# Two transformer blocks on one core: weight pieces issued as the ones before them land, and modulation rows and scan results placed in later levels of the token steps

## The reference

```python
mod = jax.nn.silu(c) @ ada_w[l] + ada_b[l]
sh1, sc1, g1, sh2, sc2, g2 = [m[:, None, :] for m in jnp.split(mod, 6, axis=-1)]
hx = modulate(rms_norm(x, norm1_g[l]), sh1, sc1)

def step(S, inp):
    r_t, w_t, kk_t, b_t, v_t, k_t = inp
    sa = jnp.einsum("bhvk,bhk->bhv", S, kk_t)
    S = (S * w_t[:, :, None, :] - sa[..., None] * b_t[:, :, None, :]
         + v_t[..., None] * k_t[:, :, None, :])
    return S, jnp.einsum("bhvk,bhk->bhv", S, r_t)

for d in range(N_DIR):
    state, y = wkv_scan(init[d], rh, to_heads(decay), kk, kk * to_heads(a), vh, to_heads(k_d),
                        reverse=(d == 1))
    y_sum = y if y_sum is None else y_sum + y
```

## Time and profile before

| | us |
|---|---|
| median of 3 runs | 1566.41 (1563.55 to 1569.16) |
| the profiled execution, its own time | 1571.56 |
| its span, first to last instruction | 1570.0 |
| PE busy | 1489.1 |
| DVE busy | 920.6 |
| ACT busy | 597.5 |
| POOL busy | 272.7 |
| mean granted TensorE clock, share of full speed | 0.962 |

### The profile page before, as it was taken

The page is one execution under the profiler, slowest core; times in us unless marked ns, Lnnn a source line. Parts: engine busy times, 40 slices in busy tenths (PEclk is TensorE's granted clock), DMA queues, the critical chain, the costliest instruction groups (busy, mean ns, idle before and its releaser), DMA issues.

```text
span 1570.0 us, 35522 instructions
## 1 busy us (share of the span) xinstructions
PE 1489.1 (95%) x14858; PEld 1227.3 (78%) x14858; DVE 920.6 (59%) x1499; ACT 597.5 (38%) x1037; POOL 272.7 (17%) x290
## 2 busy tenths in 40 slices
PE   5999988999999989999999998998989999999997
PEld 3788865788899777887777887877878888888885
DVE  4424245588667748888886224767565655555222
ACT  4422344435342534444443223546664222322221
POOL 0000023565352010111111121000021111111110
PEclk9999997789879999999999999999999999999999
DMA  9232201233220222232223222221112232232221
GB/s 372 96 109 81 81 0 50 63 95 103 81 64 4 83 81 81 81 107 82 105 87 104 92 92 81 98 72 55 59 50 87 102 107 91 96 107 92 93 92 72
DMA packets 38987, 139.15 MB, mean 89 GB/s; under 512 B 3152, under 2 KB 3664, under 8 KB 38480
## 3 DMA queue, kind: packets, MB, share of 16 engines
q1 hardware_dynamic: 38720, 135.24, 25.4%
q10 hardware_dynamic: 144, 2.10, 0.3%
HBM read 135.22 MB, written 2.10 MB: 87 GB/s over the span
## 4 chain that ended last, share of the span: by engine, by line
PE 79%; DVE 13%; ACT 3%; issue 3%; DMA 1%; ACTq 0%; DVEq 0%; SPq 0%
PE bank L722 56%; PE bank L904 9%; DVE ffn_sb L3159 5%; PE bank L731 2%; PE bank L668 2%; PE bank L998 1%; DVE w_up L2587 1%; PE bank L1070 1%; PE bank L1010 1%; DMA arena<-w 1%; PE bank L935 1%; PE bank L661 1%; ACT w_up L1681 1%; ACT arena L2177 1%; DVE w_in L2587 1%
## 5 line engine op out<-in xcount | busy, mean ns | idle before, releaser
L722 PE MATMUL bank<-hf_hi,w_up 128*128 128x512 f32 x1376 | 424.0, 389 | 0.0
L722 PEld LDWEIGHTS bank<-hf_hi,w_up 128*128 128x128 f32 x1376 | 258.3, 188 | 53.2
L722 PE MATMUL bank<-hf_lo,w_up 128*128 128x512 f32 x688 | 269.1, 391 | 4.6 <-DVE w_up L2587 4.6
L722 PE MATMUL bank<-act_hi,w_down 128*128 128x512 f32 x704 | 216.7, 389 | 0.0
L904 PEld LDWEIGHTS bank<-arena 64*64 64x64 f32 x4224 | 161.1, 154 | 31.6 <-issue 19.3
L904 PE MATMUL bank<-arena 64*64 64x32 f32 (+1 forms) x4224 | 172.4, 237 | 7.8 <-DVE arena L2814 2.5
L1681 ACT ACTIVATE w_up<-ring 128x1024 fp32r<-128x1024 f32 x87 | 91.9, 1058 | 215.7 <-PE bank L722 215.7
L2587 DVE TENSOR_TENSOR w_up<-ring,w_up 128x1024 fp32r<-128x1024 f32 x87 | 106.8, 1229 | 97.0 <-ACT w_up L1681 97.0
L722 PEld LDWEIGHTS bank<-hf_lo,w_up 128*128 128x128 f32 x688 | 129.1, 188 | 36.1 <-DVE w_up L2587 8.8
L3159 DVE SCALAR_TENSOR_TENSOR ffn_sb<-ffn_sb 128x512 f32<-128x512 f32 x176 | 151.5, 861 | 5.4
L722 PEld LDWEIGHTS bank<-act_hi,w_down 128*128 128x128 f32 x704 | 132.1, 188 | 27.3
(11 more groups left out here) (350 smaller groups left out, 2388.8 us busy)
## 6 DMA issues: line engine op xcount, KB each, us to landing
ring<-w SPq DMA_DIRECT2D x76, 1024.0 KB, 4.8
ring<-w SPq DMA_DIRECT2D x32, 704.0 KB, 4.0
ring<-w SPq DMA_DIRECT2D x64, 256.0 KB, 3.0
arena<-w SPq DMA_DIRECT2D x8, 1024.0 KB, 18.2
x<-xT SPq DMA_DIRECT2D x1, 2048.0 KB, 10.2
x<-xT ACTq DMA_DIRECT2D x1, 2048.0 KB, 8.4
outT<-x SPq DMA_DIRECT2D x4, 512.0 KB, 2.7
arena<-ctxT SPq DMA_DIRECT2D x1, 1024.0 KB, 18.4
```

The lines of the kernel that those rows point to most:

```text
L722: ins = mm(out, w[:, a, k, :], of_block(b, k0 + k), start=first and k == 0 and m == 0, stop=last and k == n - 1 and m == 2)
```

## The change

Three things are changed.

1. `load_paced` no longer goes by the levels of the scan. The 8 pieces of a step go round by round: the first piece of either slot waits until PE has used the slot, and every further piece waits until the piece before it in its own slot has landed. The two slots take turns, so at most two pieces are under way. `pace` is gone.
2. The PE loop over n = 2 to 10 is split in two. For n = 2 to 6 the rows move back: `ada_part(n, 0)` behind `nx(m, 0, 5)`, `ada_part(n, 1)` behind `dx(m, 0, 5)`, `ada_select(n)` behind `dx(m, 0, 6)`. For n = 7 to 10, which have no rows, the results move back: `results(n, 0)` behind `dx(m, 0, 4)`, `results(n, 1)` behind `dx(m, 0, 5)`.
3. ACT's `first_result(n, 1)` moves ahead of `ada_row_out(n)` and `state_padded(m, 1)`.

```diff
-            def load_paced(g, at, m, u):
-
-                sp.wait_ge(s["product"], DONE[g - 2])
-                to = ring[:, g % 2, :].rearrange("p (c n) -> p c n", c=2)
+            def load_paced(m):
+
                 for e in range(PARTS):
-                    step, l = pace(m, u, e)
-                    sp.wait_ge(s[("nx_mm0", "dx_mm0")[l % 2]], 5 * step + l // 2 - 1)
                     c, half = e // 2, slice(KB * P // 2 * (e % 2), KB * P // 2 * (e % 2 + 1))
-                    sp.dma_start(to[:, c, half], w8[2 * at + c][:, half]).then_inc(s[f"slot_in{g % 2}"], 16)
+                    for u in range(2):
+                        g = PACED[2 * m + u]
+                        at = 21 + g - SLOT["ADA2"]
+                        to = ring[:, g % 2, :].rearrange("p (c n) -> p c n", c=2)
+                        if e == 0:
+                            sp.wait_ge(s["product"], DONE[g - 2])
+                        else:
+                            sp.wait_ge(s[f"slot_in{g % 2}"], 16 * (LANDED[g] - PARTS + e))
+                        sp.dma_start(to[:, c, half], w8[2 * at + c][:, half]).then_inc(s[f"slot_in{g % 2}"], 16)
...
-            for n in range(NCC - 2, NC - 1):
+            for n in range(NCC - 2, 7):
                 m, q = n + 1, n + 2
...
                 results(n, 1)
-                ada_part(n, 0)
                 dx(m, 1, 4)
                 nx(m, 0, 5)
-                ada_part(n, 1)
+                ada_part(n, 0)
                 nx(m, 1, 5)
                 dx(m, 0, 5)
+                ada_part(n, 1)
                 dx(m, 1, 5)
                 nx(m, 0, 6)
+                nx(m, 1, 6)
+                dx(m, 0, 6)
                 ada_select(n)
+                dx(m, 1, 6)
+            for n in range(7, NC - 1):
...
+                nx(m, 0, 4)
+                turned(m, 1)
+                nx(m, 1, 4)
+                dx(m, 0, 4)
+                results(n, 0)
+                dx(m, 1, 4)
+                nx(m, 0, 5)
+                nx(m, 1, 5)
+                dx(m, 0, 5)
+                results(n, 1)
+                dx(m, 1, 5)
+                nx(m, 0, 6)
                 nx(m, 1, 6)
                 dx(m, 0, 6)
                 dx(m, 1, 6)
...
                 tok_out(m, 0)
+                first_result(n, 1)
                 ada_row_out(n)
                 state_padded(m, 1)
-                first_result(n, 1)
                 state_padded(m, 0)
```

More of the change, by code:

```diff
@@ L630, in _ @@
             for m in range(8):
-                for u in range(2):
-                    g = PACED[2 * m + u]
-                    load_paced(g, 21 + g - SLOT["ADA2"], m, u)
+                load_paced(m)
             sp.wait_ge(s["bh0"], 2 * NCC)
@@ L1271, in _ @@
                 results(n, 1)
-                ada_part(n, 0)
                 dx(m, 1, 4)
                 nx(m, 0, 5)
-                ada_part(n, 1)
+                ada_part(n, 0)
                 nx(m, 1, 5)
                 dx(m, 0, 5)
+                ada_part(n, 1)
                 dx(m, 1, 5)
                 nx(m, 0, 6)
+                nx(m, 1, 6)
+                dx(m, 0, 6)
                 ada_select(n)
+                dx(m, 1, 6)
+            for n in range(7, NC - 1):
+                m, q = n + 1, n + 2
+                nx(m, 0, 2)
+                updates(n, 0)
+                nx(m, 1, 2)
+                scores(q, 0)
+                dx(m, 0, 2)
+                dx(m, 1, 2)
+                state_terms(n, 0)
+                if n == NC - 2:
+                    gate_products(0, 1)
+                updates(n, 1)
+                nx(m, 1, 3)
+                nx(m, 0, 3)
+                scores(q, 1)
+                dx(m, 1, 3)
+                turned(m, 0)
+                dx(m, 0, 3)
+                state_terms(n, 1)
+                if n == NC - 2:
+                    gate_products(1, 2)
+                nx(m, 0, 4)
[10 more added lines that the diff above has]
+                nx(m, 0, 6)
                 nx(m, 1, 6)
```

## The result

The changed kernel takes 1570.33 us, the median of 20 runs (1563.94 to 1574.71), against 1563.74 us for the kernel before (20 runs, 1556.07 to 1569.68). The ratio is 1.0038, with a 95% interval of 1.0023 to 1.0053: 0.4% slower, where 1555 and faster was forecast. The profiled execution took 1572.13 us, of which 1570.4 are the span; before, these were 1571.56 and 1570.0. Its mean granted clock is 0.966, and it was 0.962.

A forecast was written before the change was run, and what follows sets the result against it. PE, busy 1489.1 of 1570.0 us, was taken as the bound. 1571.6 - 19.2 (clock) + 2.0 + 3.2 (order) = 1557.6; for the median run 1557.6 or 1552.4, middle 1555 (chance 0.75), range 1548 to 1565.

The forecast's parts named there:

- the order: Moved PE groups in steps 2 to 10: +2.0 us in steps 2 and 3, 0 in 4 to 6, +3.2 in 7 to 10.
- the clock term: Wide products late in scan steps keep PE's clock from falling to half: -19.2 us, bounds 0 and -19.2.
- one long fall: Profiled execution lies 5.2 us above the median run, about one long clock fall; if so, the median had fewer to lose.
- no stretch of 13.6 us at 0.50 between 340 and 520: Sign in the changed profile that the forecast is right: no such long half-clock stretch of PE there.
- Order, steps 7 to 10: Second moved result group adds 1.1 us, level 5 gains 0.3: +0.8 a step, 3.2 in four; bounds -0.3 and 2.2 a step.
- PE's idle time ahead of `nx(m, 1, 5)`: Sign in the changed profile: PE idle some 0.5 us there in steps 7 to 10.
- the results lose their cover: Rival: DVE ends level 4, so moved results are exposed on PE in full; 1577 if the clock gains nothing; chance 0.04.
- Order, steps 2 and 3: Second row product comes where nobody waits and adds 1.0 us a step, +2.0 in all; bounds 0 and 1.0 a step.
- About 1.2 us: Sign in the changed profile: PE idle this long before `dx(m, 1, 4)` of steps 2 and 3.
- Order, steps 4 to 6: Rows change places with groups PE has to do in any case, no new wait: 0.
- Pieces: Steady pair of weight loads, no row product waits: 0, between -0.8 and +0.8 us a step, 4 us either way.
- The rival of the pieces that hold up PE's instructions: Two pieces always under way cost 0.8 us more in each of five steps, 1559; chance 0.04.

The follow-up runs named there:

- r_pieces: Kernel before with only the change's new issue of the weight pieces, PE's order as before: 1565.5 us, ratio 1.0025.
- r_old_pieces: The change with weight pieces issued as before and POOL writing direction 1's decayed result rows behind the keys: 1557.2 us, ratio to before 0.9954.
- r_pool: The change with POOL's decayed result rows of direction 1 moved behind the keys: 1560.4 us, ratio to before 0.9983.
- r_back1: Kernel before with results of steps 7 to 10 moved, but `results(n, 1)` right behind `results(n, 0)`, POOL's order as before: 1562.3 us, ratio 1.0005.
- r_results_pool: Kernel before with the results of steps 7 to 10 moved and POOL's direction 1 result rows behind the keys: 1559.8 us, ratio 1.0004.
- r_best: Kernel before with rows of steps 4 to 6 and results of steps 7 to 10 moved, POOL's direction 1 result rows behind the keys: 1561.1 us, ratio 0.9979.
- r_results: Kernel before with only the results of steps 7 to 10 moved, and ACT's order there as in the change: 1567.7 us, ratio 1.0032.
- r_rows: Kernel before with only the rows of steps 2 to 6 moved: 1561.8 us, ratio 1.0000.
- r_rows4: Kernel before with only the rows of steps 4 to 6 moved: 1559.9 us, ratio 0.9982.
- r_late1: Against r_results, `results(n, 1)` three groups later still in steps 7 to 10: 1581.6 us, ratio to before 1.0115, 6 runs.

## Why the prediction was wrong

The terms of the sum came to -19.2 for the clock and +5.2 for the order, -14.0; the medians moved by +6.6. Of these 20.6 us the clock term holds 16.1 and the rest 4.6. Two steps failed, the clock's size and the order in steps 7 to 10, and they don't weigh the same. With the clock term at its measured -3.1, the forecast order alone gives +2.1: the oversized clock term is enough to turn the sign. With only the order as measured, the sum would still be -9.4.

**Clock, -19.2 us: the direction was right, the size was not.** The time at half clock (twice 1 minus the mean clock, times the span) is 102.8 us on average over before's 99 runs, and 94.1 in the change's 20. At 0.36 us each that gives back 3.1 us. Two things went wrong here. I took the falls of one execution as fixed to their places, but r_pieces has the same order of products and none of the three long falls. The profiled execution, at 0.962, was below before's mean of 0.9671. The prediction saw that it might be "one long fall" off and still took off two of three. And it did not see that the change would bring new falls. Its sign of being right, no stretch of 13.6 us at 0.50 between 340 and 520, fails twice, from 359.8 and from 462.3:

```profile
360.00:373.40 13.40, 13.40 (x243) 10.97 (x237) 6.44 (x20) 6.16 (x17) 3.63 (x6) 0.50 0.44 125
462.40:475.90 13.50, 13.50 (x231) 12.54 (x223) 7.66 (x19) 2.29 (x8) 4.55 (x7) 0.50 0.02 4
```

The idea itself holds in part: with the waits repaired, r_old_pieces has 78.3 us at half clock and r_pool 80.2, where before has 102.8; at 0.36 that is 8 to 9 us. The fourteen profiles, one execution each, say where. In steps 7 to 9 they bear it out. Six of them have the results in their old place, and in five of these (all but r_pieces) a stretch of 6.8 to 13.7 us at 0.50 begins 3 to 5 us ahead of the scores of step 8. In the 4 us before it PE stands idle for 0.84 us at most, and in the profile of before not at all. None of the five with late results and no idle time ahead of the scores (r_back1, r_pool, r_results_pool, r_best, r_old_pieces) has one in these steps. In steps 4 to 6, which carried 9.9 of the 19.2 us, nothing is seen of it. The two long falls stand in the profile of before alone. The other six with these rows in their old place have none to two short ones of 3.4 us, and so have the seven with them moved. In steps 2 and 3 five of nine profiles have stretches at 0.50 with the rows in their old place, and one of five (the change) with them moved, too few to decide.

**Order, steps 7 to 10, +0.8 a step: a wait that was not in it.** This step looked only at who ends the levels, PE or DVE, and asked what the moved group covers on PE. The group also gives a buffer free, and who waits for that is POOL. The earlier trace rows stood in the prediction as a stretch in which the clock might fall; it was also the cover of POOL's chain, with 0.4 us to spare. The term was sized 3.2 us; at the same clock r_results measures 6.2, of which 4.3 are the two waits. And they took back clock: r_pool, without them, has a mean clock 0.0043 higher than the change, another 4.9 us, so part of what the clock term lacks is theirs. With POOL mended, r_results_pool measures 1.6, so the part that was seen is even under the 3.2. PE's idle time ahead of `nx(m, 1, 5)` was forecast as 0.5 us in steps 7 to 10; step 9 shows 0.59, steps 7 and 8 none. The rival of the other side, "the results lose their cover", had the right moved group and the wrong mechanism: no group of results is exposed in full.

**Order, steps 2 and 3, +2.0: nearly right.** About 1.2 us was forecast ahead of `dx(m, 1, 4)`; the changed kernel has

```profile
337.53 0.25 PE L900 MATMUL bank<-arena 64*64 64x32 f32 x2 [1.57 <-DVE arena L2798]
...
357.94 0.25 PE L900 MATMUL bank<-arena 64*64 64x32 f32 x2 [1.18 <-DVE arena L2798]
```

r_rows against r_rows4 gives 4.7 us for the two steps at the same clock, 3.7 by their own sessions, each with a standard error of about 1; the idle times add up to 2.7.

**Order, steps 4 to 6, 0: right** (r_rows4, -0.5). **Pieces, 0, 4 us either way: inside its bounds**, but on the slow side: 2.5 to 3.0 us in r_pieces, 0.7 to 2.1 between r_pool and r_old_pieces. The rival of the pieces that hold up PE's instructions, with a chance of 0.04, leans the same way. PE never waited for a slot: between 240 and 530 us of the changed profile `ada_part` (L664) has no idle time ahead of it. The landing times did not tell it, 2.4/3.1/5.0 us against 2.4/3.0/4.3 in the earlier trace rows.

**The sum** by what was measured: -3.1 for the clock, and +9.8 at the same clock for +5.2 forecast, is +6.7 us; the medians differ by 6.6. That these agree proves nothing, as the +9.8 was worked out from the times and the clock. In the two profiles PE's idle time grows by 8.2 us: 4.3 (scores), 2.2 (rows of steps 2 and 3) and 3.3 ("issue"), with 1.6 less elsewhere. The three parts by themselves are +6.2 (results), +4.1 (rows) and +3.0 (pieces), 13.3 in all, which is more than the 9.8 of the change; why they don't add up is open.

## What to carry to other kernels

A group of instructions that is moved later also frees its inputs later. Follow the buffer to the engine that refills it and on to the next reader, and compare that chain with the work left between the two on the waiting engine, before costing the group itself. Where the wait is then named "issue", look at the other engines' timelines at that moment.

Where a clock moves the time by chance, one profile cannot carry a clock term. Compare kernels by their mean clock over many runs and, apart from that, at the same clock; a part that costs 5 us and one that gives 5 us back can otherwise be read as one that does nothing.

## What the runs showed of the hardware

The granted clock fell behind short stands of PE. The three kernels with waits ahead of the scores have six of them in their profiles, 1.8 to 4.0 us long. Behind five, a stretch at 0.50 began 0.1 to 1.5 us after PE resumed: at 462.3 in the change, at 454.1 and 478.0 in r_results, at 466.1 and 490.0 in r_late1. The first lasted 13.6 us, the last 10.2; all but the start of it:

```profile
490.30:500.40 10.10, 10.10 (x174) 9.56 (x167) 5.30 (x12) 0.76 (x2) 0.72 (x1) 0.51 0.01 3
```

The wait of 1.78 us in the change was followed by none. The four kernels with late results and mended POOL order (r_pool, r_results_pool, r_best, r_old_pieces) have no stretch at 0.50 in steps 8 and 9, nor has r_back1. The Trainium skill (TensorE: Matmul & The Clock Gate, HAM oscillation) ties falls of the clock to PE standing idle. These waits agree with it, though four of the six are of 1.8 to 2.5 us and its example has waits of about 3 to 5. The prediction had set that page against the earlier trace rows, where the clock fell without a gap. Both happen in this kernel, and close to the same place: five kernels with early results have their fall 3 to 5 us ahead of the scores of step 8, behind idle times of 0 to 0.84 us.

How much the waits move the mean clock is shown best by the change and r_pool (0.9700 and 0.9743). r_results and r_results_pool (0.9693 and 0.9704) can't be told apart. The 0.9593 of r_late1 can't be put down to its longer waits: in steps 8 and 9 its profile has 13.6 us at 0.50, as much as that of r_results, and the rest of its stretches lie elsewhere. What decides where the falls without idle time come was not found.
